# Third block's constants taken at other places of the second MLP, and weights' parts made two products ahead

## The chip, the cores and the metric

The kernel runs on one core of a Trainium2 chip, as one program. The metric is the time of one execution on the device in microseconds (us), as the median of several runs.

## The reference

Three transformer-like blocks follow each other on one sequence of 1024 tokens with 1024 features, all in float32. Cut to what matters here:

```
x = x + square(relu(rms_norm(x) @ w_up)) @ w_down                  # end of block 1, 1024 -> 4096 -> 1024 ("first MLP")

u = causal_dwconv(rmsnorm(x) @ w_up_2)                             # end of block 2 ("second MLP")
x = x + (silu(u[:, :2816]) * u[:, 2816:]) @ w_down_2

mod = silu(c) @ w_ada + b_ada                                      # block 3, one row of 6 x 1024
shift1, scale1, gate1, shift2, scale2, gate2 = split(mod, 6)
h = rms_norm(x) * (1 + scale1) + shift1;  z = h @ w_in_3
...
h = rms_norm(x) * (1 + scale2) + shift2
f = square(relu(h @ w_fc1)) @ w_fc2                                # "third MLP"
```

Block 3's `mod` doesn't depend on x, and neither does what its two shifts give behind the next weights: `shift1 @ w_in_3` and `shift2 @ w_fc1`. The kernel computes these rows beside the MLPs of blocks 1 and 2. They are called constants here: 48 pieces of `mod` ("ada") in the first MLP and 44 pieces of the two shift rows ("b") in the second.

## The kernel before

Features lie on partitions and tokens along the free axis, so a product takes one tile of weights (128 outputs, up to 1024 inputs) against all 1024 tokens and fills one of three PSUM slots. Float32 products are made of three products of reduced-precision parts: weights and activations are each split into a high part and a low part, and TensorE computes high x high, high x low and low x high (L552, L553, L558, in `job`). For every weight tile that takes three steps ahead of the product: SyncE loads it to one of four slots `raw` (L2536), ScalarE rounds it to one of two buffers `whi` (the high part, L1092), and GpSimd writes the difference over the raw tile (`wlo`, the low part, L2342; `raw` and `wlo` are the same memory). A high buffer is free when the product two before has ended; a slot when its user is done.

The order is written out by hand. One list, `stream`, holds all weight tiles in the order of use. Tiles of the constants stand in it too, but are not split and no product reads them. Every engine walks the same plan. An MLP's plan (`mlp_plan`) has groups of up products, each of which gives one tile of hidden activations, and groups of eight down products, which add into X; the up products of group g+1 stand ahead of the down products of group g. The first MLP has eight groups of four up products. The second has groups of 2, 4, 4, 4, 4 and 4, an up item being a pair of products (`fupa`, `fupb`) with a convolution and a gate behind; its down products have 2 tiles of hidden activations in the first group and 4 in the others. The items of a plan are numbered by n. In the second MLP the down products of the six groups are n = 6 to 13, 18 to 25, 30 to 37, 42 to 49, 54 to 61 and 62 to 69.

`ADA_AT` and `ROW_AT` say behind which items a constant is taken, one at each. A constant takes five steps: SyncE loads 512 KB of weights to a slot; GpSimd multiplies them in place with the vector (`row_tile`, L2348, "tile"); VectorE sums over the inputs (`row_sum`, L1875, "reduction"), which frees the slot; TensorE sums over the partitions by two small matmuls (L722 in the first MLP, L999 in the second, "row product"), which stands behind the product of the next item. In the first MLP VectorE has the reduction ahead of the same item's drain, in the second behind it.

SyncE loads in the order of the stream, four entries ahead, and each load waits until its slot is free (the product that used it, or the reduction). ScalarE and GpSimd make parts by `behind(name)`: at the item of a product they make what is still missing up to two entries further in the stream, entries of constants counted. Behind that, ScalarE's `after_row` and a `lows(widx[name] + 3)` on GpSimd (behind the tile) go one entry further where the next entry is a constant. GpSimd then has, for an up product, the low half of the hidden activations (GL, L2348); ScalarE the high half (GH, L1283 and L1521), from VectorE's drain in T.

Of the kernel before, what the change touches and what calls it, by code (L numbers as in the profile page):

```python
# [23 lines left out]
ADA_AT = sorted([0, 1, 2] + [n for n in range(4, 88) if (n - 4) % 12 in (0, 1, 2, 5, 7, 9)] + [15, 27, 39])  # L24
ROW_AT = [n for n in range(3, 62) if n % 4]
LEVELS = (64, 32, 16, 8, 4, 2, 1)
# [218 lines left out]
def build(nc, d, out):  # L245
    ctx = ExitStack()
    with ctx:
# [150 lines left out]
        wl = stream(d)  # L398
# [680 lines left out]
        def scalar(e):  # L1079
# [14 lines left out]
            def behind(name):  # L1094
                highs(widx[name] + 2)

# [171 lines left out]

            def mlp(up, dn, sizes, norm, pre, bias=None, first_copy=None, after=None, on_last=None, rt_free=()):

# [14 lines left out]
                for what, g, j in mlp_plan(up, dn, sizes):  # L1285
                    if what == "up":
                        f = 4 * g + j
                        behind(f"{up}{f}")
                        if after:
                            after(f"{up}{f}")  # L1290
                        if f == 0:
# [7 lines left out]
                    else:  # L1299
                        behind(f"{dn}{g}_{j}")  # L1300
                        if after:
                            after(f"{dn}{g}_{j}")
                        if g == 0 and first_copy:
# [7 lines left out]

            def after_row(name):

                i = widx[name] + 1
                if i < len(wl) and not wl[i][2]:
                    highs(i + 2)

            def on_last3(m):
# [5 lines left out]

            mlp("up", "dn", [4] * 8, "n2", [pe("wo7")], after=after_row, on_last=on_last3)

# [204 lines left out]
            for what, g, j in mlp_plan("fup", "fdn", SIZES2):  # L1531
                if what == "up":
# [6 lines left out]
                    behind(f"fupb{m}")  # L1539
                    after_row(f"fupb{m}")  # L1540
                    if m == 0:
# [3 lines left out]
                else:  # L1545
                    behind(f"fdn{g}_{j}")
                    after_row(f"fdn{g}_{j}")
                    if g == 5 and j:
# [782 lines left out]
        def gpsimd(e):  # L2331
# [12 lines left out]
            def behind(name):  # L2344
                lows(widx[name] + 2)

# [79 lines left out]
            def row_step(n, name):  # L2426
                if n in ADA_AT:
                    f = ADA_AT.index(n)
                    row_tile(f"ada{f}", SC[:], ac("sc"))
                    lows(widx[name] + 3)  # L2430

# [38 lines left out]
            def row2_step(n, name):  # L2470
                if n in ROW_AT:
                    f = ROW_AT.index(n)
                    row_tile(f"b{f}", mod[:, 0:8] if f < 12 else mod[:, 24:32], dv("mod"))
                    lows(widx[name] + 3)

# [373 lines left out]
```

## Time and profile before

| | |
|---|---|
| median of 3 runs | 3813.86 us (3811.79 to 3815.37) |
| profiled execution | 3815.13 us, its span 3813.3 us |
| TensorE (PE) busy | 3604.0 us, 95% of the span |
| VectorE (DVE) / ScalarE (ACT) / GpSimd (POOL) busy | 1614.5 / 997.3 / 1250.8 us |
| TensorE's granted clock, mean | 0.953 |
| chain of work that ended last | PE 89%, DVE 6%, ACT 2%, POOL 1% |

An engine's busy time is the time that its instructions took; an idle engine that is not the bottleneck costs nothing. The chain of work that ended last is followed back from the last instruction, at each step to what released it. It runs over TensorE for 89% of the span, so what counts is where TensorE waits, and for whom. The first MLP lies at about 555 to 1275 us of the span, the second at about 2000 to 2750.

### The profile page before, as it was taken

The numbers are of one execution on the slowest core, as the hardware profiler recorded it, in microseconds if no ns is written. First come the engines' busy times: TensorE is split into PE (matmuls) and PEld (weight loads), VectorE is DVE, ScalarE is ACT, GpSimd is POOL, SyncE is SP. The second block draws the span as 40 slices with busy tenths as digits, with TensorE's granted clock in tenths as the row PEclk, the third lists the DMA queues.
The fourth block names the chain that finished last, engine by engine and source line by source line (L and its number), as shares of the span: only waits on it lengthen the run. The fifth ranks groups of instructions, "written<-read, shape, count | busy, mean of one in ns | idle before, by whom it ended". The sixth has DMA issues, their size and how long they took to land.

```text
span 3813.3 us, 39574 instructions
## 1 busy us (share of the span) xinstructions
PE 3604.0 (95%) x17146; PEld 2896.4 (76%) x17146; DVE 1614.5 (42%) x1642; ACT 997.3 (26%) x1414; POOL 1250.8 (33%) x627
## 2 busy tenths in 40 slices
PE   7998899999999999998899899999998989999997
PEld 5786788888888777655688678778776768888886
DVE  4553443333333476445545444444535251222224
ACT  4331221111111311444423122122332233222211
POOL 2111325444444422100223333443425243333332
PEclk9998999999999999968999999999999989999998
DMA  2011312222222211100111222222211111111112
GB/s 95 28 51 49 111 56 70 88 91 94 83 83 75 86 61 39 51 7 3 50 50 46 82 70 77 91 72 70 86 54 34 45 69 48 47 45 50 48 50 110
DMA packets 87417, 239.81 MB, mean 63 GB/s; under 512 B 13110, under 2 KB 20038, under 8 KB 87116
## 3 DMA queue, kind: packets, MB, share of 16 engines
q1 hardware_dynamic: 87244, 237.28, 19.3%
q8 instruction: 135, 2.21, 0.2%
q14 instruction: 38, 0.31, 0.0%
HBM read 219.27 MB, written 17.97 MB: 62 GB/s over the span
## 4 chain that ended last, share of the span: by engine, by line
PE 89%; DVE 6%; ACT 2%; POOL 1%; issue 1%; DMA 0%; SPq 0%; DVEq 0%; ACTq 0%
PE ps L552 26%; PE ps L558 26%; PE ps L553 26%; PE ps L814 1%; PE ps L844 1%; PE ps L864 1%; PE ps L879 1%; DVE HL L1642 1%; PE ps L578 1%; DVE T L1651 1%; DVE T L1626 1%; POOL GL L2348 1%; PE ps L926 1%; PE ps L910 1%; PE ps L565 1%
## 5 line engine op out<-in xcount | busy, mean ns | idle before, releaser
L2342 POOL TENSOR_TENSOR wlo<-raw,whi 128x1024 fp32r<-128x1024 f32 (+3 forms) x368 | 697.8, 1896 | 1787.8 <-ACT whi L1092 1643.3
L552 PE MATMUL ps<-HH,whi 128*128 128x512 f32 (+2 forms) x2816 | 1127.1, 400 | 71.4 <-DVE HL L1642 30.1
L553 PE MATMUL ps<-HL,whi 128*128 128x512 f32 (+2 forms) x2816 | 1114.6, 396 | 0.0
L558 PE MATMUL ps<-HH,wlo 128*128 128x512 f32 (+2 forms) x2816 | 892.4, 399 | 0.0
L1092 ACT ACTIVATE whi<-raw 128x1024 fp32r<-128x1024 f32 (+3 forms) x368 | 311.0, 845 | 1857.7 <-PE ps L558 1680.2
L552 PEld LDWEIGHTS ps<-HH,whi 128*128 128x128 f32 (+2 forms) x2816 | 536.5, 191 | 199.3 <-DVE HL L1642 29.1
L552 PE MATMUL ps<-GH,whi 128*128 128x512 f32 x1536 | 610.0, 397 | 19.1 <-POOL wlo L2342 12.6
L553 PEld LDWEIGHTS ps<-HL,whi 128*128 128x128 f32 (+2 forms) x2816 | 536.6, 191 | 115.5 <-issue 2.3
L558 PEld LDWEIGHTS ps<-HH,wlo 128*128 128x128 f32 (+2 forms) x2816 | 526.1, 190 | 105.8
L553 PE MATMUL ps<-GL,whi 128*128 128x512 f32 x1536 | 602.0, 392 | 0.0
L558 PE MATMUL ps<-GH,wlo 128*128 128x512 f32 x1536 | 477.7, 392 | 0.0
L1626 DVE TENSOR_TENSOR X<-ps,X 128x1024 f32<-128x1024 f32 x184 | 225.0, 1223 | 530.6 <-PE ps L558 530.5
L552 PEld LDWEIGHTS ps<-GH,whi 128*128 128x128 f32 x1536 | 292.0, 190 | 80.0 <-POOL wlo L2342 13.7
L558 PEld LDWEIGHTS ps<-GH,wlo 128*128 128x128 f32 x1536 | 291.6, 190 | 61.6
L553 PEld LDWEIGHTS ps<-GL,whi 128*128 128x128 f32 x1536 | 291.2, 190 | 58.5
L2348 POOL TENSOR_TENSOR GL<-T,GH 128x1024 fp32r<-128x1024 f32 x86 | 206.8, 2405 | 368.9 <-ACT GH L1283 236.2
L1875 DVE TENSOR_REDUCE adat<-raw 128x128 f32<-128x1024 f32 x92 | 185.4, 2016 | 264.8 <-POOL raw L2348 264.8
L1637 DVE TENSOR_TENSOR T<-ps,RT 128x1024 f32<-128x1024 f32 x72 | 88.0, 1224 | 334.9 <-PE ps L558 296.9
L1626 DVE TENSOR_TENSOR T<-ps,RT 128x1024 f32<-128x1024 f32 (+2 forms) x34 | 41.6, 1224 | 291.1 <-PE ps L558 259.0
L1629 DVE SCALAR_TENSOR_TENSOR T<-T,cols,T 128x1023 f32<-128x1023 f32 x88 | 130.2, 1479 | 59.4 <-ACT T L1507 57.8
L1283 ACT ACTIVATE GH<-T 128x1024 fp32r<-128x1024 f32 x64 | 67.9, 1061 | 268.9 <-DVE T L1626 268.9
L1626 DVE TENSOR_TENSOR T<-T 128x1024 f32<-128x1024 f32 (+3 forms) x74 | 112.7, 1523 | 40.2 <-ACT T L1275 39.1
(339 smaller groups left out, 3034.4 us busy)
## 6 DMA issues: line engine op xcount, KB each, us to landing
raw<-in_w_up SPq DMA_DIRECT2D x76, 512.0 KB, 3.4
raw<-in_w_in SPq DMA_DIRECT2D x70, 512.0 KB, 3.4
raw<-in_w_fc SPq DMA_DIRECT2D x64, 512.0 KB, 3.4
raw<-in_w_down SPq DMA_DIRECT2D x104, 256.0 KB, 2.7
raw<-in_w_ada SPq DMA_DIRECT2D x48, 512.0 KB, 3.6
raw<-in_w_fc SPq DMA_DIRECT2D x64, 256.0 KB, 2.7
X<-in_xT SPq DMA_DIRECT2D x16, 512.0 KB, 6.5
raw<-in_w_out SPq DMA_DIRECT2D x16, 512.0 KB, 3.3
```

The source lines that it names most:

```text
L552: e.matmul(o_[0:m, half(hf)], whi_[:, k, :], hi[k0 + k][:, half(hf)], start=first, stop=False)
L553: e.matmul(o_[0:m, half(hf)], whi_[:, k, :], lo[k0 + k][:, half(hf)], start=False, stop=False)
L558: i = e.matmul(o_[0:m, half(hf)], wlo_[:, k, :], hi[k0 + k][:, half(hf)], start=False, stop=last)
L565: i = e.matmul(misc[:, 512 + b:513 + b], T[2][:, blk(b)], ones[:, 0:1], start=(b == 0), stop=True, skip_group_check=True)
L1092: e.activation(whi_of(name), raw_of(name), ACT.Copy).then_inc(*ac.inc("hi " + name))
L1283: e.activation(GH[:, sl, :], t[:], ACT.Copy).then_inc(*ac.inc(f"{up}hi{f}"))
L1626: e.tensor_tensor(o, a, b, op).then_inc(*dv.inc(*names))
L1629: e.scalar_tensor_tensor(out=o, in0=a, scalar=s_, in1=b, op0=op0, op1=op1).then_inc(*dv.inc(*names))
L1637: e.tensor_tensor(dst, ps[slot[g]][:], RT[:], MUL).then_inc(*dv.inc("free " + g, *names))
L1875: e.tensor_reduce(adat[:, f % 2, :], raw_of(name).rearrange("p (k m) -> p m k", k=8), AX.X, ADD).then_inc(*dv.inc("red " + name))
L2342: e.tensor_tensor(wlo_of(name), raw_of(name), whi_of(name).bitcast(F), SUB).then_inc(*po.inc("lo " + name))
L2348: e.tensor_tensor(o, a, b, op).then_inc(*po.inc(*names))
```

## The change

Constants in the second MLP are taken at other items. Before, at n = 3 to 61 except every fourth. Now at n = 2, 3, 4; at the first three up items of the next four groups (14 to 16, 26 to 28, 38 to 40, 50 to 52); at the first seven down products of three groups (18 to 24, 30 to 36, 42 to 48) and at all eight of the fifth (54 to 61). The first, short group of down products (6 to 13) has none. There are 44 on both sides. Those of the first MLP stay where they are.

`behind` makes parts up to the second next product, however many constants stand between. The steps of one entry more, `after_row` and `lows(widx[name] + 3)`, are gone, in both MLPs.

```diff
-ROW_AT = [n for n in range(3, 62) if n % 4]
+ROW_AT = [n for n in range(2, 62) if n < 5 or 14 <= n < 53 and (n - 14) % 12 < 3
+          or n >= 18 and (n - 18) % 12 < 8 and n not in (25, 37, 49)]
...
             def behind(name):
-                highs(widx[name] + 2)
+                highs(widx[cut[min(cidx[name] + 2, len(cut) - 1)]])
...
-            def after_row(name):
-
-                i = widx[name] + 1
-                if i < len(wl) and not wl[i][2]:
-                    highs(i + 2)
-
...
-            mlp("up", "dn", [4] * 8, "n2", [pe("wo7")], after=after_row, on_last=on_last3)
+            mlp("up", "dn", [4] * 8, "n2", [pe("wo7")], on_last=on_last3)
...
             def behind(name):
-                lows(widx[name] + 2)
+                lows(widx[cut[min(cidx[name] + 2, len(cut) - 1)]])
...
                     row_tile(f"ada{f}", SC[:], ac("sc"))
-                    lows(widx[name] + 3)
...
                     row_tile(f"b{f}", mod[:, 0:8] if f < 12 else mod[:, 24:32], dv("mod"))
-                    lows(widx[name] + 3)
```

`cut` is the list of split tiles' names and `cidx` a name's place in it. What this makes of the queues stands below at three places; the number at a name is its buffer (58 to 61 and 54 to 57 are the same four slots as `wlo` and as `raw`).

GpSimd in the second MLP, the first down products of the second group (n = 18 and on), before. The first row is the last up product's low half; a row with `mod` is a constant's tile:

```order
L2348 TENSOR_TENSOR GL<-T_66,GH 128x1024
L2342 TENSOR_TENSOR wlo_59<-raw_55,whi_63 128x512
L2348 TENSOR_TENSOR raw_54<-raw_54,mod 128x1024
L2342 TENSOR_TENSOR wlo_61<-raw_57,whi_62 128x512
L2348 TENSOR_TENSOR raw_56<-raw_56,mod 128x1024
L2342 TENSOR_TENSOR wlo_58<-raw_54,whi_63 128x512
```

And in the changed kernel:

```order
L2331 TENSOR_TENSOR wlo_60<-raw_56,whi_62 128x512
L2331 TENSOR_TENSOR wlo_58<-raw_54,whi_63 128x512
L2337 TENSOR_TENSOR GL<-T_66,GH 128x1024
L2331 TENSOR_TENSOR wlo_60<-raw_56,whi_62 128x512
L2337 TENSOR_TENSOR raw_57<-raw_57,mod 128x1024
L2331 TENSOR_TENSOR wlo_58<-raw_54,whi_63 128x512
L2337 TENSOR_TENSOR raw_55<-raw_55,mod 128x1024
```

The low parts of the first two down products moved ahead of GL. Behind GL comes now the third product's, then the first constant's tile, and so on: the tile of constant n stands behind the low part of product n+2, where it stood behind that of n+1.

SyncE's queue in the second MLP, the loads of the same group before (`in_w_down` is a down product's tile, `in_w_fc` and `in_w_in` are constants'):

```order
L2536 DMA raw_57<-in_w_down 128x512
L2536 DMA raw_54<-in_w_in 128x1024
L2536 DMA raw_55<-in_w_down 128x512
L2536 DMA raw_56<-in_w_fc 128x1024
L2536 DMA raw_57<-in_w_down 128x512
L2536 DMA raw_54<-in_w_down 128x512
```

And in the changed kernel:

```order
L2523 DMA raw_56<-in_w_down 128x512
L2523 DMA raw_57<-in_w_in 128x1024
L2523 DMA raw_54<-in_w_down 128x512
L2523 DMA raw_55<-in_w_in 128x1024
L2523 DMA raw_56<-in_w_down 128x512
L2523 DMA raw_57<-in_w_in 128x1024
L2523 DMA raw_54<-in_w_down 128x512
```

Product and constant take turns now, seven times in a row. The last row but one is constant n+2's load, into the slot of constant n, and the last is product n+3's, behind it.

GpSimd in the first MLP, up products of a group whose constants are rows with `SC`, before:

```order
L2348 TENSOR_TENSOR GL<-T_67,GH 128x1024
L2342 TENSOR_TENSOR wlo_61<-raw_57,whi_63 128x1024
L2348 TENSOR_TENSOR raw_56<-raw_56,SC 128x1024
L2348 TENSOR_TENSOR GL<-T_65,GH 128x1024
L2342 TENSOR_TENSOR wlo_59<-raw_55,whi_62 128x1024
L2348 TENSOR_TENSOR raw_54<-raw_54,SC 128x1024
L2342 TENSOR_TENSOR wlo_60<-raw_56,whi_63 128x512
```

And in the changed kernel:

```order
L2337 TENSOR_TENSOR GL<-T_67,GH 128x1024
L2331 TENSOR_TENSOR wlo_59<-raw_55,whi_62 128x1024
L2337 TENSOR_TENSOR raw_56<-raw_56,SC 128x1024
L2337 TENSOR_TENSOR GL<-T_65,GH 128x1024
L2331 TENSOR_TENSOR wlo_60<-raw_56,whi_63 128x512
L2337 TENSOR_TENSOR raw_54<-raw_54,SC 128x1024
```

The low parts moved up by one against tiles and GL: `wlo_59` and `wlo_60`, each of the product two ahead, stand ahead of the tile that they stood behind.

## Rows read from the trace of the kernel before

**Rows 1.** Waits of TensorE, 560 to 1275 us: waiter, released by; total, times, longest (us).
```profile
PE ps L552 <- DVE T L1629: 2.4, 1, 2.4
```
**Rows 2.** Waits of TensorE, 2090 to 2740 us.
```profile
PE ps L999 <- DVE adat L1875: 19.8, 8, 5.7
PE ps L552 <- POOL wlo L2342: 18.2, 7, 5.6
```
**Rows 3.** Timeline of TensorE, second MLP: start us, us, instruction, [idle before <-releaser].
```profile
2155.99 0.79 PE L552 MATMUL ps<-HH,whi 128*128 128x512 f32 x1 [5.64 <-POOL wlo L2342]
...
2258.41 0.79 PE L552 MATMUL ps<-GH,whi 128*128 128x512 f32 x1 [2.50 <-POOL wlo L2342]
```
**Rows 4.** Timeline of VectorE, second MLP: drains, additions to X, a reduction.
```profile
2111.90 1.22 DVE L1637 TENSOR_TENSOR T<-ps,RT 128x1024 f32<-128x1024 f32 x1 [5.71 <-PE ps L558]
...
2247.22 1.23 DVE L1637 TENSOR_TENSOR T<-ps,RT 128x1024 f32<-128x1024 f32 x1 [6.06 <-PE ps L558]
...
2272.53 1.22 DVE L1626 TENSOR_TENSOR X<-ps,X 128x1024 f32<-128x1024 f32 x1 [2.53 <-PE ps L558]
2278.21 1.22 DVE L1626 TENSOR_TENSOR X<-ps,X 128x1024 f32<-128x1024 f32 x1 [4.46 <-PE ps L558]
...
2283.66 1.23 DVE L1626 TENSOR_TENSOR X<-ps,X 128x1024 f32<-128x1024 f32 x1 [2.29 <-PE ps L558]
...
2300.71 1.22 DVE L1626 TENSOR_TENSOR X<-ps,X 128x1024 f32<-128x1024 f32 x1 [4.46 <-PE ps L558]
...
2535.60 1.94 DVE L1875 TENSOR_REDUCE adat<-raw 128x128 f32<-128x1024 f32 x1
...
2669.64 1.23 DVE L1637 TENSOR_TENSOR T<-ps,RT 128x1024 f32<-128x1024 f32 x1 [5.71 <-PE ps L558]
...
2727.47 1.23 DVE L1626 TENSOR_TENSOR X<-ps,X 128x1024 f32<-128x1024 f32 x1 [2.35 <-PE ps L558]
```
**Rows 5.** Timeline of SyncE's queue, second MLP: loads of down products' weights.
```profile
2255.87 6.72 SPq L2536 DMA_DIRECT2D raw<-in_w_down  x2
...
2537.94 0.43 SPq L2536 DMA_DIRECT2D raw<-in_w_down  x1
```
**Rows 6.** Timeline of ScalarE, second MLP: the high parts of those loads.
```profile
2259.41 0.63 ACT L1092 ACTIVATE whi<-raw 128x512 fp32r<-128x512 f32 x1 [4.18 <-DMA raw<-in_w_down]
...
2541.79 0.63 ACT L1092 ACTIVATE whi<-raw 128x512 fp32r<-128x512 f32 x1 [4.50 <-DMA raw<-in_w_down]
```
**Rows 7.** Timeline of GpSimd, second MLP: GL, a low part, a tile.
```profile
2254.79 2.35 POOL L2348 TENSOR_TENSOR GL<-T,GH 128x1024 fp32r<-128x1024 f32 x1 [8.79 <-ACT GH L1521]
...
2542.50 1.29 POOL L2342 TENSOR_TENSOR wlo<-raw,whi 128x512 fp32r<-128x512 f32 x1 [0.23 <-ACT whi L1092]
2543.75 1.90 POOL L2348 TENSOR_TENSOR raw<-raw,mod 128x1024 f32<-128x1024 f32 x1
```
**Rows 8.** Timeline of SyncE's queue, first MLP: loads of up products' weights.
```profile
578.46 0.81 SPq L2536 DMA_DIRECT2D raw<-in_w_up  x2
...
782.68 0.33 SPq L2536 DMA_DIRECT2D raw<-in_w_up  x1
```
**Rows 9.** Timeline of ScalarE, first MLP: a high part that waited for its load.
```profile
786.24 1.06 ACT L1092 ACTIVATE whi<-raw 128x1024 fp32r<-128x1024 f32 x1 [8.11 <-DMA raw<-in_w_up]
```
**Rows 10.** Timeline of GpSimd, first MLP: its low part.
```profile
787.38 2.39 POOL L2342 TENSOR_TENSOR wlo<-raw,whi 128x1024 fp32r<-128x1024 f32 x1 [4.92 <-ACT whi L1092]
```
**Rows 11.** Timeline of VectorE, first MLP: drains, and a reduction.
```profile
581.53 1.23 DVE L1629 SCALAR_TENSOR_TENSOR T<-ps,RT 128x1024 f32<-128x1024 f32 x1 [5.08 <-ACT RT L1131]
...
704.81 1.23 DVE L1629 SCALAR_TENSOR_TENSOR T<-ps,RT 128x1024 f32<-128x1024 f32 x1
...
717.10 1.21 DVE L1629 SCALAR_TENSOR_TENSOR T<-ps,RT 128x1024 f32<-128x1024 f32 x1
...
791.66 2.01 DVE L1875 TENSOR_REDUCE adat<-raw 128x128 f32<-128x1024 f32 x1 [6.01 <-POOL raw L2348]
```
**Rows 12.** A window: length, busy us (instructions) of PE, PEld, DVE, ACT, POOL; clock.
```profile
2257.00:2264.00 7.00, 5.59 (x13) 4.43 (x14) 1.99 (x1) 0.63 (x1) 6.30 (x5) 0.52 0.34 120
```

More of the change, by code:

```diff
@@ L1267, in scalar, with mlp @@
             square("n2", 7, X[:, 7, :])
-            def mlp(up, dn, sizes, norm, pre, bias=None, first_copy=None, after=None, on_last=None, rt_free=()):
+            def mlp(up, dn, sizes, norm, pre, bias=None, first_copy=None, on_last=None, rt_free=()):
                 def drain(f):
@@ L1288, in mlp @@
                         behind(f"{up}{f}")
-                        if after:
-                            after(f"{up}{f}")
                         if f == 0:
@@ L1300, in mlp @@
                         behind(f"{dn}{g}_{j}")
-                        if after:
-                            after(f"{dn}{g}_{j}")
                         if g == 0 and first_copy:
@@ L1539, in scalar @@
                     behind(f"fupb{m}")
-                    after_row(f"fupb{m}")
                     if m == 0:
@@ L1546, in scalar @@
                     behind(f"fdn{g}_{j}")
-                    after_row(f"fdn{g}_{j}")
                     if g == 5 and j:
```

## The prediction

> **What bounds the kernel now.** TensorE does. I read the two MLPs that the change touches: first who waited for whom, then the timelines of the engines that feed TensorE. In the first MLP TensorE waits once, 2.4 us at its start [rows 1]. In the second it waits 19.8 us before row products, for VectorE's reductions, and 18.2 us before products, for GpSimd's low parts [rows 2]. These 38 us are what there is to gain. They lie at the start of each group of down products: in the short first group from 2111.90 (the last up product's drain starts) to 2155.99 (the next up product begins), 44.1 us [rows 3, 4], and once in each later group: from the drain at 2247.22 to the last down product's at 2300.71 it is 53.5 us, though eight down products take 8 x 5.45 = 43.6. A down product takes 5.45 us (2278.21 to 2283.66), 5.68 with a row product between (2272.53 to 2278.21) [rows 4]; so an up product, with twice the matmuls, takes 10.9 us and a row product 0.2.
>
> **What the lead of two products does to the order.** There are two high buffers, so the high part of product n+2 can't be made before product n has ended; the change makes no part earlier than that. It changes what stands behind it. Before, GpSimd has at product n the low part of n+1, whose high part has long been there, then constant n's tile, then the low part of n+2. Now the low part of n+2 comes first and the tile stands behind it. So the tile of constant n, its reduction on VectorE and its row product, which TensorE has right behind product n+1, start only after product n has ended; before, they were done by then. On ScalarE a high part and a copy to GH change places, 1 us each, which costs nothing by itself. No instruction and no byte is added.
>
> **Second MLP, a down product with a constant.** SyncE loads in stream order, and a constant's slot comes free with its reduction. The load of product n+3 stands behind the load of constant n+2, which waits for the reduction of constant n. On product n+3's load hang its high part, its low part, then the tile of constant n+1 and its reduction: a closed ring from one reduction to the next. In the rows: a reduction ends at 2535.60 + 1.94 = 2537.54 [rows 4], the second of two loads goes out at 2537.94 [rows 5], the high part starts at 2541.79, as the DMA lands [rows 6], the low part at 2542.50, the tile at 2543.75 for 1.90 [rows 7], a reduction takes 2.0. A turn is 4.25 + 0.71 + 1.25 + 1.90 + 2.0 = **10.1 us**, against 5.68 now. With the fastest such load (2255.87 to 2259.41, 3.54 us instead of 3.85 [rows 5, 6]) it is 9.8. Before, the tile doesn't stand behind the low part that hangs on the ring, so one turn covers two products, 5.05 us each, just under 5.68: that is why it doesn't show.
>
> **Second MLP, by group.** Count from the start of the last up product's drain. Its low half GL starts 7.57 us later and takes 2.35 (2254.79 against 2247.22 [rows 4, 7]), so GpSimd is free at 9.9. Low part of the third down product 1.25, tile 1.9, reduction 2.0: the first reduction ends at 15.1; TensorE wants it at 10.7 and waits 4.4. Five turns later, at 65.6, comes the sixth. The seventh hangs on the next up product's load of 512 KB: 3.56 from issue to high part, 1.14 to the low part, 4.28 to the reduction, 2.01 [rows 8 to 11], together 11.0, so 76.6. The next up product starts at 76.8 instead of 53.5: +23.3. A wait of that kind leaves some 7 us of lower clock, which cost half of it (0.52 granted in 2257 to 2264 [rows 12]); one such stretch is in the 53.5 too, the other products here lie under the ring, and I add 2 for the longer wait. Three groups: 3 x 25.3 = **+76**.
> The fifth group has a constant behind each of its eight products, the last reduction hanging on a half-size load: 15.1 + 6 x 10.1 + 9.8 = 85.5. The second product behind the group starts at 85.7, where it is 2727.47 - 2669.64 = 57.8 at the most now [rows 4]: **+28**.
> The first group has no constants any more. Eight products of half length are 21.8 us. The third still waits for GL and its own low part (9.9 + 0.7, half of 1.25 taken as an estimate, less 5.4: 5.2), the up product behind the group 0.8 for its low part (1.14 + 4.28 - 1.9 = 3.5 against 2.7), and 3 for the clock: 30.8 instead of 44.1, **-13**. The 15 constants at up products (of 44) are free, a pair of up products gives 22 us for each. Sum of the second MLP: +91. The waits of 38 us aren't taken off again, since the new starts stand in their place.
>
> **First MLP.** Its places stay, the order moves at its 48 constants. At an up product the reduction ends 3.56 + 1.14 + 4.28 + 2.01 = 11.0 us after the product (load into the slot that it leaves, high part, low part and tile, reduction [rows 8 to 11]); TensorE wants it at 10.7: wait 0.3. The loop from drain over GH, GL, low part, tile and reduction to the next drain takes 12.3 us already now (704.81 to 717.10 [rows 11]), longer than the 11.1 of a product, but starts early enough. Now it starts at the limit: the second ends at 23.3 against 22.2, wait 1.1; the third, with a half-size low part, at 34.5 against 34.4, 0.1. The second down product's low part then stands behind GL, 12.3 - 4.28 - 2.01 = 6.0 for drain to GL and 1.25 of its own behind the third reduction: 41.9 against 40.2, wait 1.7. Three down products follow with a constant each: 0.1 + 0.71 + 1.25 + 1.9 + 2.0 = 6.0 against 5.25, 0.75 each, 2.2. A group has 0.3 + 1.1 + 0.1 + 1.7 + 2.2 = 5.4, seven groups 38, and 1 more for three groups with a constant at the eighth down product. At the start of the MLP the first up product's drain stands behind the second constant's reduction, which now ends 11.0 after 578.46 [rows 8]: the drain starts at 589.5 instead of 581.53 [rows 11], and the third up product waits for its PSUM slot: 8.0, and 2.4 of lower clock. First MLP: **+49**. The third MLP and the projections have no constants; two products ahead are two queue entries there, and nothing moves.
>
> **Sum.** 3815.1 (the profiled execution's time, its span is 3813.3) + 91 + 49 = 3955. The execution lies 1.3 above the median of the runs, so 3954.
>
> **A rule beside the rows.** Right behind a wait that ends at 2258.41 [rows 3] the granted clock is 0.52, mostly 1.2 GHz [rows 12]. The Trainium skill, page "TensorE: Matmul & The Clock Gate", section "HAM oscillation — how this bites in real kernels", says that a loop whose products of one step are shorter than its wait for the next data falls back to the halved clock in every step. [...]
>
> **Rivals.**
> *Lower clock in the stalled groups.* TensorE idles 4.4 of 10.1 us in some 25 turns. If it stays at 1.2 GHz, a product takes 10.9 instead of 5.45 us and ends 11.2 after the reduction that let it go, 1.1 later than the next reduction; the load that needs its slot goes 1.1 later: 25 x 1.1 = 28, and seven waits of over 1 us in the first MLP would cost 1.5 each, 10. That gives 3992. For it: rows 12. Against: a product that fills over 9 of 10.1 us leaves the engine hardly idle, and the clock rises. Chance 0.12.
> *The first MLP absorbs it.* Its waits are 0.1 to 1.7 us beyond a limit. If the parts come 0.8 earlier than I have it, all but the start's 10 and the 1.7's remainder (6) go, some 30: 3924. Chance 0.15.
> *The ring does not bind and the starts are cured: faster.* Should the tile of constant n+1 be ready without the low part of n+3, the second MLP would lose its 38 us of waits [rows 2] and 3 us of lower clock at each of five starts: 3815 - 53 = 3762. The point from which it decides is a turn of 5.68 us against my 10.1. Against: GpSimd's queue is in order, and the rows of the change show the tile behind. Chance 0.03.
> *The change does nothing that shows*, since two high buffers forbid a real lead of two. It would hold if all tiles kept their place; they don't. 3814, chance 0.02.
>
> **How the numbers follow.** My forecast has 0.68. Its own bounds: turns of 9.8 us take 8 off; a first reduction or a limit in the first MLP may err by 1 us each, some 20 either way. The range 3905 to 4000 takes in that and the two slower neighbours; under 0.1 is left out beside the last two rivals. About 0.2% is what a measurement of this kernel can tell from none: slower by over that 0.95, within it 0.02, faster 0.03.
>
> **What would show it.** In the changed profile TensorE's waits for VectorE's reductions in the second MLP grow from 19.8 to over 90 us; reductions follow each other by 10 us in four stretches of down products, and SyncE waits for them; the short group lasts some 31 instead of 44 us; in the first MLP the third up product starts 8 us later, and row products at down products wait some 0.8. It is wrong if the reductions of the down products come every 5.7 us, or if a tile runs before the low part ahead of it in the order.

## The result, and the profile after

The changed kernel takes 3975.81 us (median of four runs, 3964.77 to 3989.66) against 3812.99 for the kernel before: 1.043 times as long, 95% interval 1.039 to 1.047. On another chip it took 3972.16 (3971.61 to 3973.01), 1.042 times (1.0405 to 1.0436). The forecast was 3954, in a range of 3905 to 4000.

The profiled execution is the longest of the four, 3989.66 us with a span of 3987.9, so 174.6 above the span before. On VectorE's timeline I cut both traces at the same instructions: the first drain of the first MLP (581.53 us before, 589.03 after), the first instruction of the second block (1281.60, 1355.69), the first convolution step of the second MLP (2002.12, 2080.19) and the end of that MLP (2782.90, 2954.80). "Again" is the profiled execution on the other chip.

| stretch, us | before | after | again | after less before | forecast |
|---|---|---|---|---|---|
| up to the first drain of the first MLP | 581.5 | 589.0 | 587.9 | +7.5 | in the next |
| first MLP | 700.1 | 766.7 | 762.6 | +66.6 | +49 with the start |
| second block up to its MLP | 720.5 | 724.5 | 714.6 | +4.0 | 0 |
| second MLP | 780.8 | 874.6 | 871.1 | +93.8 | +91 |
| the rest | 1030.4 | 1033.1 | 1033.6 | +2.7 | 0 |

The chain of work that ended last ran over PE for 89% before. In the page of after its shares are:

```profile
PE 73%; DVE 10%; POOL 9%; ACT 4%; DMA 4%; issue 1%; SPq 0%; ACTq 0%; DVEq 0%
```

VectorE, GpSimd, ScalarE and the loads now hold 27% of it, where they held 9% before. Line numbers have shifted: L553, L554 and L559 are the products' matmuls, L723 and L1000 the row products, L1093 the high part, L2331 the low part, L2337 GL and the tile, L1864 the reduction, L2523 the load.

TensorE's waits in the first MLP, 560 to 1350 us, answer to [rows 1]; columns as there (waiter, released by; total, times, longest):

```profile
PE ps L723 <- DVE adat L1864: 22.3, 31, 2.3
PE ps L553 <- POOL wlo L2331: 18.2, 9, 2.4
PE ps L553 <- DVE T L1618: 10.5, 1, 10.5
```

And in the second MLP, 2100 to 2920 us, against [rows 2]:

```profile
PE ps L1000 <- DVE adat L1864: 83.7, 29, 4.1
PE ps L553 <- POOL wlo L2331: 6.2, 2, 5.2
```

The waits before row products went from 19.8 to 83.7 us (the prediction wanted over 90); those for low parts fell from 18.2 to 6.2, which is what the change gained. The ring can be followed in one turn. Timelines of SyncE's queue, ScalarE, GpSimd (two rows) and VectorE (three rows) in the second group of down products:

```profile
2321.76 1.90 DVE L1864 TENSOR_REDUCE adat<-raw 128x128 f32<-128x1024 f32 x1 [5.56 <-POOL raw L2337]
...
2323.70 0.33 SPq L2523 DMA_DIRECT2D raw<-in_w_in  x1
2324.07 0.43 SPq L2523 DMA_DIRECT2D raw<-in_w_down  x1
...
2327.55 0.63 ACT L1093 ACTIVATE whi<-raw 128x512 fp32r<-128x512 f32 x1 [10.08 <-DMA raw<-in_w_down]
...
2328.26 1.28 POOL L2331 TENSOR_TENSOR wlo<-raw,whi 128x512 fp32r<-128x512 f32 x1 [6.53 <-ACT whi L1093]
2329.50 1.90 POOL L2337 TENSOR_TENSOR raw<-raw,mod 128x1024 f32<-128x1024 f32 x1
...
2331.43 1.90 DVE L1864 TENSOR_REDUCE adat<-raw 128x128 f32<-128x1024 f32 x1 [6.64 <-POOL raw L2337]
...
2383.44 1.93 DVE L1864 TENSOR_REDUCE adat<-raw 128x128 f32<-128x1024 f32 x1 [7.94 <-POOL raw L2337]
```

A reduction ends at 2323.66 and frees the slot; 0.04 us later the constant's load goes out, and the product's load behind it at 2324.07. High part, low part, tile, reduction follow, and the next reduction ends at 2333.33: a turn of 9.7. Each of these steps starts as the one ahead of it ends. From the first to the seventh reduction it is 61.7 us, 10.3 each; the forecast had five of 10.1 and one of 11.0, 61.5. The turns are 9.7, 9.9, 11.5, 9.9, 9.8 and 11.0: an ordinary one is shorter than the forecast's, and the one of 11.5 has a load that took 5.3 us instead of 3.5 to 3.7, so that the close sum is in part luck. TensorE waited 4.04 us before the first row product (forecast 4.4):

```profile
2323.72 0.38 PE L1000 MATMUL ps<-ones,adat 128*128 128x1 f32 x2 [4.04 <-DVE adat L1864]
```

### The profile page after: what moved, and what is told of

Same layout as the page of the kernel before. It is cut to its first block, busy times and chain, and to the rows that moved or that the text cites. A ratio compares the mean times of both kernels' runs of the same rounds, so it can differ in the third digit from the quotient of the medians.

```text
span 3987.9 us, 39583 instructions
## 1 busy us (share of the span) xinstructions
PE 3679.1 (92%) x17146; PEld 2935.6 (74%) x17146; DVE 1635.8 (41%) x1642; ACT 998.3 (25%) x1414; POOL 1270.5 (32%) x627
## 4 chain that ended last, share of the span: by engine, by line
PE 73%; DVE 10%; POOL 9%; ACT 4%; DMA 4%; issue 1%; SPq 0%; ACTq 0%; DVEq 0%
PE ps L553 21%; PE ps L559 21%; PE ps L554 21%; DVE adat L1864 3%; POOL raw L2337 3%; POOL wlo L2331 3%; DMA raw<-in_w_down 2%; POOL GL L2337 2%; DMA raw<-in_w_up 1%; ACT whi L1093 1%; PE ps L815 1%; DVE T L1615 1%; PE ps L845 1%; PE ps L865 1%; DVE T L1618 1%
## 5 line engine op out<-in xcount | busy, mean ns | idle before, releaser
L2331 POOL TENSOR_TENSOR wlo<-raw,whi 128x1024 fp32r<-128x1024 f32 (+3 forms) x368 | 698.0, 1897 | 1997.9 <-ACT whi L1093 1853.7
L553 PE MATMUL ps<-HH,whi 128*128 128x512 f32 (+2 forms) x2816 | 1133.5, 403 | 77.5 <-DVE HL L1631 29.9
L554 PE MATMUL ps<-HL,whi 128*128 128x512 f32 (+2 forms) x2816 | 1120.4, 398 | 0.0
L559 PE MATMUL ps<-HH,wlo 128*128 128x512 f32 (+2 forms) x2816 | 895.9, 400 | 0.0
L1093 ACT ACTIVATE whi<-raw 128x1024 fp32r<-128x1024 f32 (+3 forms) x368 | 311.2, 846 | 2111.9 <-PE ps L559 1554.1
L553 PEld LDWEIGHTS ps<-HH,whi 128*128 128x128 f32 (+2 forms) x2816 | 539.7, 192 | 207.2 <-DVE HL L1631 28.6
L553 PE MATMUL ps<-GH,whi 128*128 128x512 f32 x1536 | 627.0, 408 | 25.8 <-POOL wlo L2331 19.4
L554 PEld LDWEIGHTS ps<-HL,whi 128*128 128x128 f32 (+2 forms) x2816 | 540.2, 192 | 116.8 <-issue 2.9
L554 PE MATMUL ps<-GL,whi 128*128 128x512 f32 x1536 | 617.9, 402 | 0.0
L559 PEld LDWEIGHTS ps<-HH,wlo 128*128 128x128 f32 (+2 forms) x2816 | 528.0, 191 | 106.4
L559 PE MATMUL ps<-GH,wlo 128*128 128x512 f32 x1536 | 491.3, 402 | 0.0
L1864 DVE TENSOR_REDUCE adat<-raw 128x128 f32<-128x1024 f32 x92 | 181.5, 1973 | 673.0 <-POOL raw L2337 673.0
L553 PEld LDWEIGHTS ps<-GH,whi 128*128 128x128 f32 x1536 | 302.3, 197 | 92.3 <-issue 22.2
L559 PEld LDWEIGHTS ps<-GH,wlo 128*128 128x128 f32 x1536 | 301.0, 196 | 65.3
L554 PEld LDWEIGHTS ps<-GL,whi 128*128 128x128 f32 x1536 | 300.7, 196 | 61.8
L2337 POOL TENSOR_TENSOR GL<-T,GH 128x1024 fp32r<-128x1024 f32 x86 | 212.9, 2476 | 309.6 <-ACT GH L1284 211.2
L1618 DVE SCALAR_TENSOR_TENSOR T<-T,cols,T 128x1023 f32<-128x1023 f32 x88 | 163.0, 1853 | 76.5 <-ACT T L1498 74.9
```

Of the source, the lines that this page charges most:

```text
L553: e.matmul(o_[0:m, half(hf)], whi_[:, k, :], hi[k0 + k][:, half(hf)], start=first, stop=False)
L554: e.matmul(o_[0:m, half(hf)], whi_[:, k, :], lo[k0 + k][:, half(hf)], start=False, stop=False)
L559: i = e.matmul(o_[0:m, half(hf)], wlo_[:, k, :], hi[k0 + k][:, half(hf)], start=False, stop=last)
L1093: e.activation(whi_of(name), raw_of(name), ACT.Copy).then_inc(*ac.inc("hi " + name))
L1618: e.scalar_tensor_tensor(out=o, in0=a, scalar=s_, in1=b, op0=op0, op1=op1).then_inc(*dv.inc(*names))
L1864: e.tensor_reduce(adat[:, f % 2, :], raw_of(name).rearrange("p (k m) -> p m k", k=8), AX.X, ADD).then_inc(*dv.inc("red " + name))
```

## The experiments

All are compared with the kernel before, run on the same chip.

| run | us (lowest to highest) | ratio to before, 95% interval |
|---|---|---|
| the change again | 3972.16 (3971.61 to 3973.01) | 1.042 (1.0405 to 1.0436) |
| places alone | 3802.57 (3799.91 to 3803.88) | 0.9974 (0.9963 to 0.9986) |
| lead alone, old places | 3980.70 (3973.68 to 3983.69) | 1.0438 (1.0422 to 1.0453) |
| places, lead on ScalarE only | 3813.32 (3809.92 to 3817.99) | 1.0003 (0.9994 to 1.0012) |
| tile first | 3790.34 (3788.78 to 3792.29) | 0.9942 (0.9927 to 0.9956) |
| tile first, old places | 3809.21 (3804.34 to 3814.65) | 0.9992 (0.9983 to 1.0001) |
| loads swapped | 3912.70 (3908.59 to 3917.99) | 1.0265 (1.0249 to 1.0280) |
| wait filled | 3970.89 (3970.17 to 3971.97) | 1.0417 (1.0401 to 1.0432) |
| mixed | 3792.16 (3786.98 to 3793.98) | 0.9949 (0.9933 to 0.9966) |
| mixed, constants one product later | 3782.60 (3779.99 to 3782.92) | 0.9920 (0.9906 to 0.9933) |
| tile first, one product later | 3781.18 (3780.98 to 3781.82) | 0.9918 (0.9905 to 0.9932) |

**Places alone.** The kernel before with

```diff
-ROW_AT = [n for n in range(3, 62) if n % 4]
+ROW_AT = [n for n in range(2, 62) if n < 5 or 14 <= n < 53 and (n - 14) % 12 < 3
+          or n >= 18 and (n - 18) % 12 < 8 and n not in (25, 37, 49)]
```

> The kernel before with the new places of the third block's constants and nothing else. My theory: it is the lead (the tile behind the low part of product n+2) that closes the ring of 10.1 us, not the places. With the places alone the tile of a constant stands ahead of that low part, one turn covers two products (5.05 us each, under 5.68), and reductions of down products come every 5.7 us. The first MLP is as before, the short group loses its 13 us, and some of the 38 us of waits at the later groups' starts stay: 3795 to 3815, TensorE's waits for reductions in the second MLP under 30 us. Rival, the places do it: seven or eight constants in a row are more than SyncE and GpSimd feed, so the second MLP is 90 us longer here too, and the time is about 3900.

Measured: 3802.57, 0.26% faster than before. TensorE's waits in the second MLP, 2090 to 2740 us:

```profile
PE ps L553 <- POOL wlo L2343: 29.0, 6, 5.7
```

There is no wait for a reduction any more, seven constants in a row or not. The short group is 16.2 us shorter (39.3 for 55.5, from the convolution step behind the last up pair's drain to the next pair's drain), and the start of each long group keeps its 5.7 us. So the places lose nothing; they are a small gain inside a change that lost 4%.

**Lead alone.** The changed kernel with the old `ROW_AT`, the first diff reversed.

> The changed kernel with the old places of the third block's constants: the lead of two products alone. My theory: the first MLP loses the same 74 us as in the change, its lower clock of 37 us included. In the second, three of four down products have a constant, so about three turns of 10.1 us replace four products of 5.6 us (+8 for four, +16 for a full group), five such groups, less what the old starts already waited: some 50 us. Together about 3935, between 3915 and 3955. Rival, the places carry the second MLP's loss: only the first MLP's 74 us are left, 3888.

Measured: 3980.70, as slow as the whole change, 45 us more than I had expected. The rival is out; the places carry none of the loss. My sizing of the second MLP was off: it is 99 us longer than before, not 50. VectorE in one group:

```profile
2340.47 1.92 DVE L1863 TENSOR_REDUCE adat<-raw 128x128 f32<-128x1024 f32 x1
...
2350.21 1.91 DVE L1863 TENSOR_REDUCE adat<-raw 128x128 f32<-128x1024 f32 x1 [6.69 <-POOL raw L2336]
...
2358.74 1.95 DVE L1863 TENSOR_REDUCE adat<-raw 128x128 f32<-128x1024 f32 x1 [5.49 <-POOL raw L2336]
...
2373.46 1.91 DVE L1863 TENSOR_REDUCE adat<-raw 128x128 f32<-128x1024 f32 x1 [5.48 <-POOL raw L2336]
```

Four products with three constants take 9.7 + 8.5 + 14.7 = 33.0 us, where I had three turns of 10.1: a product without a constant is no pause in the ring. And the short group, which has constants here, takes 72.8 us instead of 55.5; I had given it next to nothing.

**The lead on ScalarE only.** The changed kernel, with GpSimd's order of before:

```diff
@@ GpSimd
             def behind(name):
-                lows(widx[cut[min(cidx[name] + 2, len(cut) - 1)]])
+                lows(widx[name] + 2)
...
                     row_tile(f"ada{f}", SC[:], ac("sc"))
+                    lows(widx[name] + 3)
...
                     row_tile(f"b{f}", mod[:, 0:8] if f < 12 else mod[:, 24:32], dv("mod"))
+                    lows(widx[name] + 3)
```

> The changed kernel with GpSimd's order taken back to that of before (two entries ahead, one more behind the tile); new places, and ScalarE two products ahead. It differs from the places alone only on ScalarE, where a high part and a copy to GH change places, 1 us each. My theory: that costs nothing, so its time is that of the places alone within 5 us. Rival: the high part ahead of GH makes GH, GL and all behind it late by 1 us, some 30 us more than the places alone.

Measured: 3813.32, 10.8 us more than the places alone. Neither theory had it: I said nothing, the rival said 30 us from GH and GL. The second MLP takes the same in both within 0.1 us at each cut; all of it lies at the start of the first MLP (4.1) and in it (6.9). ScalarE at that start, first with the places alone, then here:

```profile
578.80 1.02 ACT L1132 ACTIVATE RT<-ps 128x1024 f32<-128x1024 f32 x1 [10.49 <-PE ps L579]
```

```profile
581.96 1.06 ACT L1093 ACTIVATE whi<-raw 128x1024 fp32r<-128x1024 f32 x1 [10.67 <-DMA raw<-in_w_up]
582.92 1.00 ACT L1132 ACTIVATE RT<-ps 128x1024 f32<-128x1024 f32 x1
```

The high part of the product two ahead stands ahead of `RT`, on which the first drain depends, and waits for its load. TensorE's wait there grows from 2.4 to 5.2 us, a stretch of 6.8 us at the lower clock goes with it (none with the places alone), and six waits for low parts come in, 2.8 us in all.

**Tile first.** The changed kernel, with the tile ahead of the low part two products ahead; so at the down products, and in the same way at the up products and in the first MLP:

```diff
                 else:
-                    behind(f"fdn{g}_{j}")
                     row2_step(n, f"fdn{g}_{j}")
+                    behind(f"fdn{g}_{j}")
```

> The changed kernel, but GpSimd takes a constant's tile ahead of the low part of product n+2 at every item, in both MLPs. Places, ScalarE's and SyncE's orders are the change's. My theory: the order of tile and low part on GpSimd is the whole of the loss, since a tile needs only its load. Reductions come every 5.7 us, the first MLP is as before, and the second loses most of its 38 us of waits and the lower clock behind them: 3762 to 3785, faster than the kernel before by 1%. Rival 1, the low part behind the tile becomes late in turn, 1.9 us at each down product: the second MLP keeps its waits, 3815 or more. Rival 2, the ring is SyncE's alone (loads in the order of the stream): it stays at 3950 or more.

Measured: 3790.34, 182 us below the change and 0.6% below the kernel before. Nothing else was touched than which of two instructions GpSimd takes first. It is 5 us above the range that I gave. The first MLP is back at 702.9 us, the second takes 753.8, against 780.8 before. Two reductions of the second group, 5.7 us apart, which start without a wait for GpSimd:

```profile
2255.36 2.01 DVE L1864 TENSOR_REDUCE adat<-raw 128x128 f32<-128x1024 f32 x1
...
2261.04 2.00 DVE L1864 TENSOR_REDUCE adat<-raw 128x128 f32<-128x1024 f32 x1
```

Waits of TensorE in the second MLP, 2090 to 2740 us:

```profile
PE ps L1000 <- DVE adat L1864: 11.3, 4, 2.8
PE ps L553 <- POOL wlo L2331: 6.2, 2, 5.2
```

Of 38 us of waits 17.5 are left: one of 2.8 before the first row product of each long group (GpSimd has GL, then the tile, then VectorE the reduction), and the short group's 5.2.

**Tile first, old places.**

> Tile ahead of the low part in both MLPs, as in the run of that name, but with the places of before. Theory: order and places are separate and add up. The lead with the tile behind costs 177 us at the old places and 170 at the new, so the tile ahead takes nearly all of it back at either. At the old places the short group keeps the constants that the new places take from it; with the tile ahead it is 16 us longer at most, and the later groups as with the new places: 3795 to 3812. Rival: the two depend on each other, and at the old places the lead of two costs even with the tile ahead: over 3815.

Measured: 3809.21, inside the expectation and the same as before within the interval. The table of both parts (medians in us, from different chips, on which the kernel before has 3811.9 to 3813.0) says what depends on what:

| | old places | new places |
|---|---|---|
| order of before | 3812 | 3802.6 |
| two products ahead, tile behind | 3980.7 | 3972.2 |
| two products ahead, tile first | 3809.2 | 3790.3 |

The lead as the change makes it costs 169 us at the old places and 170 at the new, and the tile's place alone 171 and 182. The lead of two with the tile first gains 12 us at the new places; at the old ones it is 3, which the interval doesn't tell from nothing.

**Loads swapped.** The changed kernel; in the second MLP a down product's load goes out ahead of the constant's that stands before it in the stream:

```diff
+            for i in range(len(wl) - 1):
+                if wl[i][0].startswith("b") and wl[i + 1][0].startswith("fdn"):
+                    w_todo[i], w_todo[i + 1] = i + 1, i
...
-                while w_todo and w_todo[0] <= upto:
+                while w_todo and w_todo[0] <= upto + 1 and min(w_todo[:2]) <= upto:
```

> The changed kernel, but in the second MLP SyncE issues a down product's load ahead of the load of the constant that stands before it in the stream. All else stays, the tile behind the low part too. My theory of the ring has two links: this load behind the constant's load that waits for a reduction, and the tile behind the low part. This takes the first link away. The load of product n+3 then goes out with the end of product n, and the loop is product end, load 3.85, high and low part 2.0, tile 1.9, reduction 2.0, row product and the next product, over two products: turns of about 7.2 us in place of 10.1, some 25 of them, so 70 us off: 3895 to 3915; the first MLP stays as in the change. Rival, the reduction's own slot is what binds (a constant's load waits for a reduction anyway): turns stay at 10 us and the time within 10 us of the change.

Measured: 3912.70, inside the expectation. Reductions of one group:

```profile
2303.73 1.93 DVE L1864 TENSOR_REDUCE adat<-raw 128x128 f32<-128x1024 f32 x1 [5.56 <-POOL raw L2337]
...
2308.14 1.97 DVE L1864 TENSOR_REDUCE adat<-raw 128x128 f32<-128x1024 f32 x1 [1.35 <-POOL raw L2337]
...
2320.57 1.90 DVE L1864 TENSOR_REDUCE adat<-raw 128x128 f32<-128x1024 f32 x1 [5.26 <-POOL raw L2337]
...
2326.22 2.01 DVE L1864 TENSOR_REDUCE adat<-raw 128x128 f32<-128x1024 f32 x1 [2.62 <-POOL raw L2337]
...
2335.02 1.90 DVE L1864 TENSOR_REDUCE adat<-raw 128x128 f32<-128x1024 f32 x1 [5.26 <-POOL raw L2337]
...
2340.84 2.00 DVE L1864 TENSOR_REDUCE adat<-raw 128x128 f32<-128x1024 f32 x1 [2.79 <-POOL raw L2337]
...
2351.50 1.94 DVE L1864 TENSOR_REDUCE adat<-raw 128x128 f32<-128x1024 f32 x1 [5.71 <-POOL raw L2337]
```

Short and long turns alternate: 4.4, 12.4, 5.7, 8.8, 5.8 and 10.7 us. The pair in the middle takes 14.5 us, 7.2 each, as expected, but the six together take 47.8, 8.0 each, against 10.3 in the change. So the ring has the two links that the prediction named: the tile behind the low part, and the load behind the constant's load. Taking either away opens it, the first wholly (turns of 5.7), the second down to 8.0 on the mean. TensorE's waits for reductions in the second MLP fall from 83.7 to 54.3 us; the first MLP (762.9) is the change's.

**The change again, and the wait filled.** These two ran side by side. The second is the changed kernel with

```diff
+                if name[:2] == "dn" and name[-2:] == "_1" and name != "dn7_1":
+                    for _ in range(8):
+                        e.matmul(o_[:, 0:512], HH[:, 0, 0:P], HH[:, 0, 0:512], start=True, stop=True)
```

ahead of the wait for the low part.

> The changed kernel once more, beside the two runs that are made from it. Its first runs spread over 25 us, from 3964.8 to 3989.7; the number and length of the stretches of lower clock is the only thing that I see that can differ between them. Expected: 3965 to 3990 again, with a shorter time at a higher mean clock. Rival: the spread is an effect of the first chip, and these lie within 5 us.

> The changed kernel, with eight matmuls of 512 columns more at the second down product of the first seven groups of the first MLP, ahead of the wait for the low part. They write to the slot that the product then overwrites, take some 1.8 us and lie in the wait of 2.5 us; nothing that the kernel computes changes. Theory: the lower clock in the first MLP (37.5 us of it in the profiled run, a stretch right behind each such wait) comes from these waits, and costs half of its length. With the wait filled the seven stretches go, 27 us of lower clock, so 12 us off in the first MLP, and its length falls from 774 to 762 us. Rival, the lower clock comes from the short waits before row products, or is not tied to these waits: the stretches stay and the stage's length with them.

The change again: its four runs lie within 1.4 us, so this chip doesn't show the spread of 25 us; the rival came true. Its profiled execution (3971.61) is 18 us shorter than the first one at a mean clock of 0.944 instead of 0.939. Filled: the whole kernel is 1.3 us faster, no difference, but the first MLP is 756.6 us against 762.6. (The second is 8.8 us longer, 879.9 against 871.1, in which nothing was changed.) Timelines of TensorE at the wait, first in the changed kernel, with the window of 3.4 us that begins 1.3 us behind it (its columns as in [rows 12]), then filled, with the same:

```profile
668.20 0.47 PE L553 MATMUL ps<-GH,whi 128*128 128x512 f32 x1 [2.37 <-POOL wlo L2331]
...
669.50:672.90 3.40, 3.40 (x10) 2.63 (x9) 0.00 (x0) 0.00 (x0) 2.13 (x2) 0.50 0.00 0
```

```profile
664.22 1.97 PE L546 MATMUL ps<-HH 128*128 128x512 f32 x8
666.71 0.50 PE L556 MATMUL ps<-GH,whi 128*128 128x512 f32 x1 [0.52 <-POOL wlo L2334]
...
667.00:670.40 3.40, 3.40 (x16) 2.78 (x16) 0.00 (x0) 0.00 (x0) 3.24 (x2) 1.00 0.00 0
```

With TensorE at work for 1.97 of the 2.5 us, the clock stays at 2.4 GHz, and 16 instead of 10 matmuls start in 3.4 us. The clock doesn't fall behind every such wait, though. The run beside it has six waits of 2.4 us for low parts, and a stretch of 3.4 us at the lower clock stands behind four of them; a fifth stands behind a wait of 2.1 us before a row product. Behind the other two the clock stayed at 2.4 GHz, here behind the wait of 2.39 us that ends at 1157.86:

```profile
1158.10:1161.50 3.40, 3.40 (x16) 2.79 (x16) 0.00 (x0) 0.00 (x0) 3.21 (x2) 1.00 0.00 0
```

Of these stretches none is left behind the seven filled waits; one new one (941.6) stands behind a wait of 1.9 us before a row product. Together with the 10.2 us at the stage's start, 27.3 us at the lower clock became 13.6. Half of the difference is 6.8, close to the 6.0 by which the stage got shorter. The cause is confirmed, the size only half of what I expected, since that run had five such stretches and not the seven of the first profile.

**Mixed.** Places and tile first, in the second MLP alone; the first MLP in the order of before on ScalarE and GpSimd (so on both):

```diff
             def behind(name):
+                if name[:2] in ("fu", "fd"):
+                    lows(widx[cut[min(cidx[name] + 2, len(cut) - 1)]])
+                else:
+                    lows(widx[name] + 2)
```

> The new places and, in the second MLP alone, parts two products ahead with a constant's tile ahead of the low part; the first MLP in the order of before on ScalarE and GpSimd. Put together from what each part gave: the places alone are 9.5 us faster than before; in the second MLP the tile ahead with the lead of two is 12 us shorter still; and the first MLP gets back the 8 us (2.8 at its start) that ScalarE's lead of two costs there. Expected 3780 to 3792, the fastest of all. Rival: what the lead of two costs on ScalarE in the first MLP has its like in the second, and the time is that of the tile taken first, 3790, or more.

Measured: 3792.16, at the upper end of what I expected and the same as tile first, as the rival had it, but not for the rival's reason. The second MLP is the same in both (753.7 and 753.8), and the first does get its 7.2 us back. The second block's attention between them, whose instructions are the same, takes 720.5 us instead of 715.0. Its start in windows, mixed and then tile first:

```profile
1280.80:1300.00 19.20, 19.20 (x74) 16.65 (x74) 1.32 (x8) 1.62 (x3) 4.70 (x2) 0.66 0.01 2
```

```profile
1288.00:1307.20 19.20, 18.70 (x99) 15.95 (x98) 1.31 (x8) 3.06 (x5) 5.67 (x3) 0.91 0.07 20
```

The granted clock is 0.66 in the one and 0.91 in the other: a stretch of 13.7 us at the lower clock against one of 3.4, half of the difference being 5.2. Of the 7.2 us that the first MLP gave, 5.5 were lost there.

**Constants one product later.** What is left in the second MLP are the waits before each group's first row product. Both kernels, mixed and tile first, with `ROW_AT` changed to

```diff
+ROW_AT = [n for n in range(2, 62) if n < 6 or 14 <= n < 53 and (n - 14) % 12 < 3
+          or n >= 18 and 0 < (n - 18) % 12 < 8]
```

> The mixed kernel (first MLP in the order of before, second with the tile ahead and two products ahead) with the seven constants of a long group at its second to eighth down product in place of the first to seventh (and the fifth group's eight so too, the one left over at the last up item of the first group). What is left of waits for reductions in the second MLP is 11.3 us in four, each before the row product of a group's first constant: GL at 9.9 us behind the drain, tile 1.9, reduction 2.0, ends at 13.8, TensorE wants it at 10.7. One product later it is wanted at 16.4. Expected: these four waits go, some 10 us, and 3 us of lower clock: 3777 to 3784. Rival: the constant at the eighth down product, whose tile and reduction then stand ahead of the next up product's parts, costs what the first one gives: 3788 to 3800.

> The same places in the kernel with the tile ahead in both MLPs. Expected: the same 10 to 13 us off its 3790, 3776 to 3783, and the same time as the mixed kernel within 4 us, since what that one saves in the first MLP it lost to lower clock in the second block's attention. Rival: as there.

Measured: 3782.60 and 3781.18, both inside the expectation. Both beat the kernel before by 0.8%, the second being the fastest run of this study. TensorE in the second MLP of the second, 2090 to 2740 us:

```profile
PE ps L553 <- POOL wlo L2331: 6.9, 8, 2.4
PE ps L1000 <- DVE adat L1864: 5.5, 1, 5.5
```

The four waits of 2.8 are gone. The one of 5.5 lies in the short group, before the row product of the constant at n = 5, and stands in the place of the wait of 5.2 for a low part that tile first has there.

## Why the prediction was right, and where it was off

**The order, right.** Without GpSimd's tile behind the low part of product n+2 there is no loss: putting it ahead takes 182 us away, undoing the places nothing.

**The ring in the second MLP, right in its size too.** +93.8 us in the profiled execution and +90.3 on the other chip, against +91. The second group takes 25.4 us more (forecast 25.3), the next three together 82.2 (78.6), the short one 16.2 less (13). By the prediction's own cut the short group takes 30.5 us where I had 30.8. The last group, which had no term, takes 3.6 more: in its last 11 us the granted clock is 0.60, in the same place before it is 1.00. So the whole stage fits to 3 us in part by luck, since errors of some 4 us to either side cancel; each long group by itself is right within 2 us. The point from which the rival of a cured start decides, a turn of 5.68, is passed only when the tile runs first; then the kernel does get faster, though 28 us less than the 3762 that I gave: 11.3 and 6.2 us of waits stay, and the first MLP ends 6.4 us later than before.

**The waits of the first MLP, right.** They sum to 51.0 us, 2.4 of them old: +48.6, where the terms of the sum without the clock are 38 + 1 + 8 = 47. Most row products at down products wait 0.57 (forecast 0.75), the second down product of most groups 2.37 (1.7), the start 8.1 longer (8.0):

```profile
681.54 0.38 PE L723 MATMUL ps<-ones,adat 128*128 128x1 f32 x2 [0.57 <-DVE adat L1864]
```

**The step that was mis-sized: what else a wait costs there.** The stage with its start got 74.1 us longer, not 49. I gave the lower clock 2.4 us. It held for 37.5 us in eight stretches, where the kernel before had none in this stage: 10.2 at the start's wait, six of 3.4 behind the waits of 2.4 us before second down products, and one of 6.8 with a wait of 2.3 us before a row product in the fifth group. Half of that is 18.8 us, an estimate; the run with the wait filled shows the cause (13.6 us of lower clock taken away, 6.0 us gained). What is left, 74.1 - 48.6 - 18.8 = 6.7, is some 0.16 for each of 41 waits. On the other chip, with 27.3 us at the lower clock, the same sum leaves 7.2. I don't take it as shown, but one gap bears it out: the matmul before the row product at 681.54 starts 0.96 us ahead of it, of which 0.57 are the wait and 0.23 the usual distance. I had seen what a wait of 2.50 us does to the clock [rows 3, 12] and put it into the second MLP, but in the first only at its start and not in its groups, where the wait that I forecast as 1.7 us came out at 2.4.

**The first rival, the lower clock in the stalled groups, out.** The clock did fall there, 0.85 on the mean from 2318 to 2386 us and 0.71 in the product behind the first wait:

```profile
2323.70:2329.50 5.80, 5.78 (x19) 4.67 (x20) 1.10 (x1) 0.63 (x1) 1.24 (x1) 0.71 0.40 136
```

The Trainium skill, page "TensorE: Matmul & The Clock Gate", section "HAM oscillation — how this bites in real kernels", tells of a loop whose products of one step are shorter than its wait for the next data, and which falls back in every step. These down products are not such a loop, and by my own forecast (5.45 us to a wait of 4.4) they were not, so the rule gave this rival no support; here it is 5.45 us to a wait of 4.04 at the most, and a stretch at the lower clock came all the same with six of this group's seven waits. I see no cost of it: the turn is set by loads, ScalarE, GpSimd and VectorE. With TensorE slower in its part of it, the turn was still 9.7, and TensorE waited 0.9 to 4.1 us for the reduction before every one of the 29 row products of the long groups. In the first MLP, where TensorE sets the pace, a stretch behind a wait of 2.4 us cost about its half.

**"On ScalarE a high part and a copy to GH change places ... which costs nothing by itself": wrong.** It costs 10.8 us when it stands alone, all at and in the first MLP. I looked for what the high part is moved past in the steady part, not at the seam, where it is moved past `RT`. In the change, where the first drain waits for the reduction that ends at 589.12, I take most of it to lie under that wait; no run separates it there.

**The rest, +4.0 and +2.7 us,** had no term. The second block's attention has the same instructions before and after. In the thirteen profiled executions it took between 710.9 and 724.5 us, the longer the lower the granted clock (0.92 to 0.89). The 4.0 go with the clock; what sets it there no run shows, and the 2.7 I didn't follow up.

**The spread of the change's first four runs** goes the same way: 3989.66, 3984.64, 3966.99 and 3964.77 us at mean clocks of 0.939, 0.941, 0.945 and 0.947. Between the two profiled executions of the change, 18 us apart, 9.9 lie in the second block's attention, 4.0 in the first MLP and 3.5 in the second. The profiled execution is the slowest of the four, which is why it lies 175 above before where the median lies 163. Why the clock differs between executions of one kernel, and why the spread on the other chip is 1.4 us, stays open.

## What to carry to other kernels

When parts are made further ahead, look in each in-order queue at what now stands behind them. A side job that needs nothing but its own load must not stand behind a part that waits for a buffer, above all if the side job's slot is what lets that buffer's load go: that is how a ring closes, and its length is the sum of its rows. Look at the seams between stages as well as at the steady loop, and price a wait of about 2 us or more on TensorE with the lower clock behind it, unless something else sets the pace there.

## What the runs showed of the hardware

- Eight matmuls of no use, 1.97 us in a wait of 2.5, kept TensorE's clock at 2.4 GHz at all seven places. Without them it fell to 1.2 for 3.4 us (10 matmuls started in 3.4 us instead of 16) behind all six waits of 2.4 us for low parts in the change's first profile, and behind four of six in its second. So the length of the wait alone doesn't decide; a wait of 1.9 us had a stretch behind it too.
- An unchanged stage of some 715 us differs by up to 14 us between profiled executions: 710.9 us at a granted clock of 0.92, 724.5 at 0.89. A small difference in the whole time between two kernels (mixed, tile first) can so hide a gain of 7 us in one stage.

```profile
1350.90:2061.80 710.90, 671.14 (x3702) 484.62 (x3701) 364.83 (x697) 243.71 (x551) 120.84 (x47) 0.92 0.11 37
```

```profile
1355.70:2080.20 724.50, 686.05 (x3701) 493.32 (x3701) 364.83 (x697) 243.90 (x551) 120.87 (x47) 0.89 0.11 37
```

The first is the run with the loads swapped, the second the change in its first profile, with the columns of [rows 12]: the time that TensorE is busy grows by 14.9 us, that of the other engines by 0.2 at the most.
